# Input laid out by features, weights laid out by units, and a crosswise first pair of column blocks with a cap on the transfers under way

## The reference, cut to what matters

```python
def first_block(x, w_in, ...):
    proj = x @ w_in[l]                              # 256x1024 @ 1024x2560
    q, k, v, g, p = jnp.split(proj, [512, 1024, 1536, 2048], axis=-1)
    q = _rope(q.reshape(b, s, 4, 128))
    k = _rope(k.reshape(b, s, 4, 128)) * 128 ** -0.5
    ret = _retention(q, k, v) ...                   # normalised, times silu(g)
    pool = _pool_mixer(p, w_pool[l], pool_scale[l])
    mix = jnp.concatenate([ret, pool], axis=-1) @ w_out[l]
    x = _layernorm(ALPHA * x + mix, ...)
    x = _layernorm(ALPHA * x + _conv_ffn(x, ...), ...)
# second_block: SwiGLU, a 9-part projection with two attention-like branches,
# attention over a memory of 256 tokens, SwiGLU
```

## Time and profile before

| | us |
|---|---|
| median of 3 runs | 1078.8 |
| lowest, highest | 1078.46, 1079.02 |
| the profiled execution | 1078.79 |
| its span, first to last instruction | 1077.0 |
| mean granted clock of TensorE | 0.999 |

### The profile page before, as it was taken

One profiled execution on the slowest core, in us unless ns is written; L12 is line 12 of the kernel. 1 busy time (PEld: TensorE's weight loads), 2 busy tenths in 40 slices (PEclk: granted clock), 3 DMA queues, 4 the chain that ended last, 5 costly groups with the idle time before them and its releaser, 6 DMA issues.

```text
span 1077.0 us, 14156 instructions
## 1 busy us (share of the span) xinstructions
PE 1069.4 (99%) x5638; PEld 918.5 (85%) x5638; DVE 728.9 (68%) x918; ACT 580.1 (54%) x768; POOL 96.5 (9%) x73
## 2 busy tenths in 40 slices
PE   9999999999999999999999999999999999999997
PEld 7888999988888888888888888888989988888886
DVE  6668778774787675468975678657668665867642
ACT  6463655553385555458754546653446556656431
POOL 2800000000000000000454510010000000000000
PEclk9999999999999999999999999999999999999999
DMA  9855665555588777555454444467446436777741
GB/s 356 296 168 172 218 195 175 180 194 196 171 274 241 243 240 232 192 200 192 156 160 153 156 156 135 140 208 261 157 168 214 147 111 216 241 244 243 244 166 40
DMA packets 142178, 211.46 MB, mean 196 GB/s; under 512 B 8176, under 2 KB 87456, under 8 KB 141984
## 3 DMA queue, kind: packets, MB, share of 16 engines
q1 hardware_dynamic: 138688, 199.13, 56.2%
q0 software_dynamic: 3136, 11.23, 3.0%
q10 hardware_dynamic: 288, 0.20, 0.1%
HBM read 203.70 MB, written 6.82 MB: 195 GB/s over the span
## 4 chain that ended last, share of the span: by engine, by line
PE 93%; DVE 3%; ACT 2%; issue 1%; DMA 1%; SPq 0%; DVEq 0%; ACTq 0%
PE ps L726 18%; PE ps L727 18%; PE ps L728 18%; PE ps L765 5%; PE ps L763 5%; PE ps L764 5%; PE ps L1039 3%; PE ps L1038 3%; PE ps L1040 3%; PE ps L862 3%; PE ps L1228 1%; PE ps L1227 1%; PE ps L1226 1%; PE ps L1102 1%; DVE rest L1882 1%
## 5 line engine op out<-in xcount | busy, mean ns | idle before, releaser
L1882 DVE TENSOR_TENSOR rest<-raw,high 128x2048 fp32r<-128x2048 f32 x131 | 306.1, 2358 | 98.0 <-ACT high L1345 97.6
L1345 ACT ACTIVATE high<-raw 128x2048 fp32r<-128x2048 f32 x131 | 247.0, 1913 | 64.3 <-DMA raw<-in_ffn_w_down_dram 33.0
L726 PE MATMUL ps<-high,xt_high 128*128 128x512 f32 x696 | 274.5, 394 | 0.0
L728 PE MATMUL ps<-high,xt_rest 128*128 128x512 f32 x696 | 271.1, 390 | 0.0
L727 PE MATMUL ps<-rest,xt_high 128*128 128x512 f32 x696 | 270.9, 389 | 0.0
L728 PEld LDWEIGHTS ps<-high,xt_rest 128*128 128x128 f32 x696 | 130.7, 188 | 27.5
L726 PEld LDWEIGHTS ps<-high,xt_high 128*128 128x128 f32 x696 | 130.8, 188 | 25.8
L727 PEld LDWEIGHTS ps<-rest,xt_high 128*128 128x128 f32 x696 | 130.8, 188 | 25.7
L1887 DVE SCALAR_TENSOR_TENSOR rest<-raw,wgain,high 128x512 fp32r<-128x512 f32 x176 | 119.1, 747 | 35.7 <-ACT high L1349 35.7
L1349 ACT ACTIVATE high<-raw,wgain 128x512 fp32r<-128x512 f32 x176 | 110.9, 716 | 9.6 <-DMA raw<-in_ffn_w_in_dram 9.6
L1038 PE MATMUL ps<-xt_high,high 128*128 128x256 f32 x288 | 81.7, 284 | 0.0
(11 more groups left out here) (375 smaller groups left out, 1651.2 us busy)
## 6 DMA issues: line engine op xcount, KB each, us to landing
raw<-in_w_in_dram SPq DMA_DIRECT2D x88, 512.0 KB, 4.4
raw<-in_ffn_w_in_dram SPq DMA_DIRECT2D x88, 512.0 KB, 4.8
raw<-in_w_up_dram SPq DMA_DIRECT2D x44, 512.0 KB, 4.7
raw<-in_ffn_w_down_dram SPq DMA_DIRECT2D x44, 512.0 KB, 4.3
raw<-in_w_down_dram SPq DMA_DIRECT2D x22, 512.0 KB, 4.3
raw<-in_w_out_dram SPq DMA_DIRECT2D x16, 512.0 KB, 4.5
raw<-in_w_mkv_dram SPq DMA_DIRECT2D x16, 512.0 KB, 4.7
turned<-blocked SPq DMA_DIRECT2D x22, 256.0 KB, 5.3
```

The costliest lines, as they stand in the source:

```text
L726: pe.matmul(out, sh, wh, start=first, stop=False)
L728: mm = pe.matmul(out, sr, wh, start=False, stop=last)
L1345: act.activation(high[:, u % SLOTS, c], raw[:, u % SLOTS, c], ACT.Copy).then_inc(unit_high, 1)
L1882: vec.tensor_tensor(rest[:, slot, c], raw[:, slot, c], high[:, slot, c].bitcast(F32), ALU.subtract).then_inc(unit_rest, 1)
```

## The change

- The host lays the input out a second time by features (`x_t`, 128 partitions, 8 chunks, 256 tokens) and all weights by units (`units`, each 128 x 2048, contiguous). The transposes of the input and their copies drop out; `xt_high` and `xt_rest` are made from the landed `xt_raw`. `x` in token rows is still needed for the residual and comes in one transfer behind unit 9.
- Units 0 to 3 are the lead (`LEAD_UNITS = 4`). `lay_units` orders them crosswise: unit 2·half + j for block j. The lead comes in 12 pieces, eight of one chunk for the first half (q, k, q, k, ...), then q, q, k, k with two chunks each. TensorE accumulates q and k in turn in the two pairs.
- SP issues piece n only when piece n - 4 has landed (`LEAD_OPEN = 4`). The input's first chunk is issued on ScalarE's queue, the other four parts on SP's, ahead of the piece of q that needs them.
- The first high part of the input is made by VectorE; two high-by-high products start before any remainder exists.
- Warming: 7 matmuls, on a 128x128 tile repeated four times.
- GpSimd waits for the last lead piece in place of unit 3. The identity is loaded after the lead. All other units come as two transfers of contiguous 4 KB rows.

```diff
-WARM = (6, 4)
+WARM = 7
+LEAD_UNITS = 4
+XT_PARTS = ((0, 1), (1, 2), (2, 4), (4, 6), (6, 8))
+LEAD_PIECES = tuple((j, k, k + 1) for k in range(4) for j in range(2)) + tuple((j, k, k + 2) for j in range(2) for k in (4, 6))
+LEAD_OPEN = 4
...
+        xt_raw = place("xt_raw", [P, KC, S], F32, area)
...
+            if name == "win1" and j < 2:
+                return UNIT[name] + 3 + j
...
+            def load_lead():
+                for n, (j, k0, k1) in enumerate(LEAD_PIECES):
+                    if n >= LEAD_OPEN:
+                        sync.wait_ge(lead_landed[n - LEAD_OPEN], 16)
+                    u = 2 * (k0 // 4) + j
+                    c = slice((k0 % 4) * NB, ((k1 - 1) % 4 + 1) * NB)
+                    for part, (x0, _) in enumerate(XT_PARTS):
+                        if part and j == 0 and x0 == k0:
+                            load_xt(part)
+                    sync.dma_start(raw[:, u, c], dram["units"][u, :, c]).then_inc(lead_landed[n], 16)
...
+                for n in range(2):
+                    c = slice(2 * n * NB, 2 * (n + 1) * NB)
+                    sync.dma_start(raw[:, slot, c], dram["units"][u, :, c]).then_inc(unit_landed[slot], 16)
...
+            load_lead()
+            for u in range(LEAD_UNITS, UNIT["end"]):
+                load(u)
+                if u == UNIT["wout1"] - 1:
+                    sync.dma_start(x[:, :, :], dram["x"].rearrange("(t p) c -> p t c", p=P)).then_inc(x_landed, 16)
...
-            pool.wait_ge(unit_landed[3], 32)
+            pool.wait_ge(lead_landed[-1], 16)
...
             pe.wait_ge(sem("warm_ready"), 1)
-            warm(WARM[0])
+            warm(WARM)
+            for n, (j, k0, k1) in enumerate(LEAD_PIECES):
+                u = 2 * (k0 // 4) + j
...
+                if n == 0:
+                    pe.wait_ge(xt_first, 1)
+                    pe.wait_ge(lead_high, 1)
+                    for tt in range(TT):
+                        xh, _, wh, _, out = lead(0, tt)
+                        pe.matmul(out, xh, wh, start=True, stop=False)
+                pe.wait_ge(lead_rest, n + 1)
+                if j == 0:
+                    pe.wait_ge(xt_rests, [part for part, (x0, x1) in enumerate(XT_PARTS) if x0 <= k0 < x1][0] + 1)
+                for k in range(k0, k1):
+                    for tt in range(TT):
+                        xh, xr, wh, wr, out = lead(k, tt)
+                        if n:
+                            pe.matmul(out, xh, wh, start=(k == 0), stop=False)
+                        pe.matmul(out, xh, wr, start=False, stop=False)
+                        mm = pe.matmul(out, xr, wh, start=False, stop=(k == KC - 1))
+                if k1 % 4 == 0:
+                    mm.then_inc(unit_used, 1)
+            full_block("win1", 2)
             pe.wait_ge(ident_landed, 16)
-            input_transposes(0)
-            warm(WARM[1])
...
-            full_block("win1", 1)
-            full_block("win1", 2)
...
-            act.dma_start(small["ident"][:, :], dram["c_ident"]).then_inc(ident_landed, 16)
+            act.dma_start(xt_raw[:, 0, :], dram["x_t"][:, 0:S]).then_inc(xt_landed[0], 16)
...
+            for n, (j, k0, _) in enumerate(LEAD_PIECES):
+                for part, (x0, _) in enumerate(XT_PARTS):
+                    if part and j == 0 and x0 == k0:
+                        input_high(part)
+                weights_high(n)
+            act.dma_start(small["ident"][:, :], dram["c_ident"]).then_inc(ident_landed, 16)
+            split[0] = LEAD_UNITS
...
+            vec.wait_ge(xt_landed[0], 16)
+            vec.tensor_copy(xt_high[:, 0, :], xt_raw[:, 0, :]).then_inc(xt_first, 1)
+            input_rest(0)
+            for n, (j, k0, _) in enumerate(LEAD_PIECES):
...
+                weights_rest(n)
+            split[0] = LEAD_UNITS
```

More of the change, by code:

```diff
@@ L162, in splits @@
             use((name, g))
-    for g in (0, 2, 1, 3):
-        use(("x", g))
     for what in "qk":
@@ L501, in _, with load_xt, load @@
         def _(sync):
[L502 to L518, removed]
+            x_t = dram["x_t"].rearrange("p (k t) -> p k t", k=KC)
+            def load_xt(n):
+                k0, k1 = XT_PARTS[n]
+                sync.dma_start(xt_raw[:, k0:k1, :], x_t[:, k0:k1, :]).then_inc(xt_landed[n], 16)
+            def load_lead():
[8 more added lines that the diff above has]
+                    sync.dma_start(raw[:, u, c], dram["units"][u, :, c]).then_inc(lead_landed[n], 16)
+            def load(u):
                 slot = u % SLOTS
@@ L553, in load_up @@
[L553 to L565, removed]
@@ L886, in warm @@
                 for _ in range(n):
[L887 removed]
+                    pe.matmul(ps[:, 7, :], warmth[:, :], warmth[:, :].unsqueeze(1).to_broadcast([P, 4, P]), start=True, stop=True)
             pe.wait_ge(sem("warm_ready"), 1)
[L890 to L895 removed]
@@ L916, in _ @@
-            mm.then_inc(unit_used, 1)
-            wait_taken(("x", 1), ("x", 3))
-            tiles = [chunk_products("win1", 0, 1, tt) for tt in range(TT)]
-            for k in range(4):
-                pe.wait_ge(*((sem("lead_rest"), k + 4) if k < 3 else (unit_rest, 2)))
-                for tt in range(TT):
-                    sh, sr, c, out, first, last = tiles[tt][k]
-                    wh, wr = high[:, 1, c:c + NB], rest[:, 1, c:c + NB]
-                    pe.matmul(out, sh, wh, start=first, stop=False)
-                    pe.matmul(out, sh, wr, start=False, stop=False)
-                    mm = pe.matmul(out, sr, wh, start=False, stop=last)
@@ L2662, with lay_units @@
             "ffn2_post": "ffn2_post_g_2"}
-_WEIGHTS = ["w_in", "w_out", "w_up", "w_down", "ffn1_w_in_2", "ffn1_w_down_2", "w_in_2", "w_branch_a_2",
-            "w_branch_b_2", "w_out_2", "w_mq_2", "w_mkv_2", "w_mo_2", "ffn2_w_in_2", "ffn2_w_down_2", "w_pool"]
+UNIT_WEIGHTS = {"win1": "w_in", "wout1": "w_out", "up1": "w_up", "down1": "w_down",
+                "upA": "ffn1_w_in_2", "downA": "ffn1_w_down_2", "win2": "w_in_2",
+                "brA": "w_branch_a_2", "brB": "w_branch_b_2", "wout2": "w_out_2",
+                "mk": "w_mkv_2", "mva": "w_mkv_2", "mvb": "w_mkv_2", "mq": "w_mq_2", "mo": "w_mo_2",
+                "upB": "ffn2_w_in_2", "downB": "ffn2_w_down_2"}
+def lay_units(weights):
+    out = np.empty((UNIT["end"], P, 4 * NB), np.float32)
+    for name, k in BLOCKS:
+        w, u = weights[UNIT_WEIGHTS[name]], UNIT[name]
+        rows = w.reshape(-1, P, w.shape[1]).transpose(1, 0, 2)
+        if name.startswith("down"):
+            for i in range(FB):
+                out[u + i] = rows[:, 2 * i:2 * i + 2, :].reshape(P, 4 * NB)
+            continue
+        for n in range(2 * k):
+            j, half = HALF_ORDER[name][n] if name in HALVES else divmod(n, 2)
+            part = rows[:, 4 * half:4 * half + 4, :]
+            if name.startswith("up"):
+                part = np.stack([part[:, :, g * FF + 256 * j:g * FF + 256 * j + 256] for g in range(2)], 2)
+            else:
+                c0 = ({"win1": WIN1, "win2": WIN2}[name][j][1] if name.startswith("win") else
+                      j * NB + {"mva": D, "mvb": D + NB}.get(name, 0))
+                part = part[:, :, c0:c0 + NB]
+            out[u + (2 * half + j if name == "win1" and j < 2 else n)] = part.reshape(P, 4 * NB)
+    return out
 def kernel(**inputs):
```

156 lines of the change are left out of this document (47 added, 109 removed).

## The result

The changed kernel takes 1086.5 us (median of 4 runs, 1084.93 to 1087.01) where the kernel before takes 1078.9 (1078.46 to 1079.02): a ratio of 1.007, 95% interval 1.0057 to 1.0082, 7.6 us slower. A second set of 5 runs gave 1086.7 against 1078.6. The forecast was 1078.9 with a range that ends at 1082.0; the measured time lies outside it.

The account below looks back on a forecast made before the run. TensorE's stream was taken to bound the kernel. From 1078.8 us: start -2.95, unit 4 +0.2, wait for the keys +2.8, giving 1078.9; range 1075.8 to 1082.0.

Parts of the forecast that it names:

- What bounds the kernel: After 20 us only TensorE's own stream sets the time; an edit wins only before that or loses where TensorE waits.
- The start: First product at 4.7 us, level rising about 7.1, lead units ending at 27.65 instead of 30.60: 2.95 us won.
- The lead's supply: Lead transfers and splits fit under 2.72 us per 12 products; cap costs nothing, up to 1 us if cover is thinner.
- Rival 4: Cap or split starves the lead by 1 to 2 us; GpSimd's lateness covers it, so it widens nothing; no chance given.
- The port: GpSimd's rotation, sharing a port with VectorE, loses three turns of 2.0 us; k transposed at 47.9, giving back all 2.95 us.
- Rival 2: A fourth lost turn in GpSimd's rotation: 1080.9 us, or 1082 with a start at 25 us; chance 28%.
- Rival 3: VectorE shut out at unit 4, which starts at 31.9 instead of 27.65: net +1.3, 1080.1 us; chance 10%.
- The wait for k: TensorE wants rotated k at 45.1 us and gets it at 47.9: a wait costing 2.8 us.
- Everything else at nothing: Longer weight rows, one residual input transfer, gate weight layout and later identity lie behind TensorE's stream and cost nothing.

Follow-up runs that it names:

- kvec2: Changed kernel without the cap, rotation tables issued behind lead piece 6, k rotated by VectorE behind unit 6's remainder: 1076.5 us, ratio 0.9981 to the kernel before.
- norot: Changed kernel without the cap and without the rotation's twelve products, one GpSimd sum each for q and k: median 1077.9 us, ratio 0.9991 to the kernel before.
- after2: The changed kernel run again, nothing altered, for a second profile and a closer median: 1086.7 us.
- kvec2_cap: kvec2 with the cap of four lead pieces put back, nothing else changed: 1078.6 us.
- tables: Changed kernel, cap kept, with GpSimd issuing the rotation's tables behind the seventh lead piece instead of the last: 1081.3 us, ratio 1.0025 to the kernel before.
- nocap: Changed kernel with the cap taken away (12 lead pieces may be under way): 1085.2 us, ratio 1.0056 to the kernel before.
- fill2: Changed kernel with twenty unused TensorE products on zeros ahead of the k transposes: 1084.3 us.
- b_units: The kernel before with the weights laid out by units and nothing else changed: 1079.6 us, ratio 1.0009.
- straight: Changed kernel without the cap and with the crosswise lead order undone, all q chunks then all k: 1078.9 us, ratio 1.0005 to the kernel before.
- kvec: Changed kernel without the cap, tables issued behind lead piece 6, k rotated by VectorE ahead of unit 6's remainder: 1078.15 us, ratio 0.9996 to the kernel before.

## Why the prediction was wrong, point by point

- **What bounds the kernel.** Right: TensorE's stream, and what delays the transposes of k delays the end by as much, within 0.2 us wherever the level stays up. When no such wait is put in, kvec2 gains 2.1 us in the median, norot 2.9 in its profiled execution and only 0.6 in its median.
- **The start.** Right in the first product, 4.68 for 4.7. The level rose at 5.5 in place of 7.1, which by the forecast's own rule is worth 0.8 us, more than the 0.5 that it allowed for; in this lead it hardly shows, since after2, where the level rose at 7.0, has unit 4 at 29.52.
- **The lead's supply: this step failed.** "I cost the cap at nothing" rested on 1 MB under way in a transfer's 3.2 us, 320 GB/s. The 3.2 us were those of the first piece of weights (issued at 1.19, used at 4.39), on a queue that was nearly empty. In the changed kernel a piece of 256 KB takes 4.6 us from issue to landing (the median of its eight), so four make about 230 GB/s, and 234 is what 10 to 13 us show. Its stated cost if thin was "up to 1 us". It was 1.8 at unit 4 (29.87 against 28.10 without the cap) and 2.1 in the median where nothing hides it (kvec2_cap against kvec2).
- **Rival 4: this failed with it.** The text said that a starved lead "widens nothing", since GpSimd is later than TensorE anyway. But GpSimd's own start hangs on the last lead piece. It came at 29.36 in place of the forecast 24.1, outside the bounds of 23.3 to 25.5, which had been set with the issue at 17.95 "the same after". This is the largest term that was wrong: 5.3 us of the 5.4 by which k missed its forecast (53.29 for 47.9). Of the 5.3, the late tables are 3.7: tables took away just these and started at 25.64. The other 1.5 are the starved lead by its second way, a first pair that was emptied at 25.6 in place of 23.3. Even without the cap the start was 25.68, just outside the bounds, because the tables took 7.7 us to land.
- **The port.** The three lost turns, 2.0 us each and 17.7 us besides were right for the changed kernel, and the last one is the sum of k, as in the kernel before. (The forecast's own parts add up to 17.8, not 17.7.) They were right by luck in part. The forecast counted remainder 4, remainder 5 and one of 7 or 8; it was 5, 6 and 8, since with the late start remainder 4 was nearly done and 6 came into the rotation. Without the cap, which was what the forecast in effect assumed, there are five (nocap): remainders 4 to 7 all met the rotation of q, and 8 that of k. And fill2 has five with the cap. Rival 2 had the mechanism, with one extra turn; its mark, k after 49.5, was met, but in the changed kernel by the late start and not by a fourth turn. Rival 3 didn't occur at unit 4: there was no wait over 0.3 us.
- **The wait for k.** The forecast had a wait of 2.8 us and let it cost 2.8. The transposes after waits of 5.2, 3.7 and 2.0 us ran at the lower level, and low stretches of 3.4 to 6.8 us cost 1.8 to 2.7 more. This term was missing from the sum; with the forecast's own wait of 2.8 us it would have added about 1.8 us, an estimate from tables, whose wait of 1.95 cost that much.
- **Everything else at nothing.** b_units bears it out for the layout to 0.1%, with an interval that reaches from 0 to 0.2%. The rest of that list wasn't tested by itself, but TensorE has no wait behind 60 us in the changed kernel but the 0.2 that it had before.

Put together from the forecast's own terms: 1078.9, plus 5.4 for k, plus 1.8 for the level, is 1086.1, and the profiled execution is a span of 1084.3 with 1.8 around it, 1086.1.

## What to carry to other kernels

When an edit brings the bounding engine forward, list each engine that was nearly late, and for each the event that releases its *first* instruction; a cap or a reordering at the start moves that event by more than it moves the bound. Price a cap on transfers under way with the time that a transfer takes among others (4.6 us here), not with that of the first one (3.2). And move the element-wise work of the two engines that share a port apart in time, or give the work to the one that has room, before counting on an earlier start: here that, with the cap off and the tables early, turned 7.6 us lost into 2.1 won. A single profile says little of how many turns are lost: the changed kernel had three twice, and fill2, the same up to that point, five.

## What the runs showed of the hardware

- **A lost turn** costs GpSimd 1.9 to 2.1 us beside a VectorE remainder of 2.29 (once 0.8), in 2 to 5 steps of 14. VectorE loses too: the remainder that begins at 45.19 in the changed kernel takes 5.85 us (the row stands above). It ends at 51.04, so it is held through GpSimd's steps up to 48.9 and gets in ahead of the sum of k.

The Trainium skill (SBUF — State Buffer, Terms) says that the two share a port pair under an exclusive lock and that the loser is blocked for a whole instruction. The runs agree: what a turn costs GpSimd is most of a remainder. Which of the two gets the next turn differs: in nocap the remainder of unit 4, which begins with the rotation, holds off its first step (3.42), here one waits for several.

- **Transfers.** Of the 16 parts of one piece in the capped lead, the last lands 1.3 to 3.2 us behind the first from the third piece on (from 5.35 to 7.22 for the third piece, of 256 KB, from 17.18 to 20.36 for the eleventh, of 512 KB). Without the cap the early pieces spread as much (5.49 to 7.39 for the third), the eleventh only from 15.63 to 16.44. A cap waits for the last part, so the transfer engines that are done stand idle: their busy share is 0.73 in 10 to 13 us, against 1.05 without the cap.
- **The level** fell behind waits of TensorE of 2.0, 2.6, 3.7 and 5.2 us, for stretches of 3.4 or 6.8 us, and didn't behind those of 1.7 (changed kernel, lead), 1.6 (straight) and 1.1 us (kvec). With the same wait of 5.2 us it was 3.4 in one execution and 6.8 in another. The moment of its first rise, read from the spacing, moved between 5.5 and 10.1 us among kernels that start alike.
